# Weights as one array of units by partition, x, p and norm vectors with features on partitions: a two-layer decoder trunk on one core

## What is computed

```python
for i in range(2):
    f = swiglu(rms_norm(h, ffn1_pre_g[i]), ffn1_w_gu[i], ffn1_w_down[i])   # 1024 -> 2*2816 -> 1024
    h = h + 0.5 * rms_norm(f, ffn1_post_g[i])
    u = rms_norm(h, mix_pre_g[i]); ...   # u @ w_in[i] (5120 columns), two attentions, two branches, w_out
    h = h + rms_norm(merged @ w_out[i], mix_post_g[i])
    f = swiglu(rms_norm(h, ffn2_pre_g[i]), ffn2_w_gu[i], ffn2_w_down[i])
    h = h + 0.5 * rms_norm(f, ffn2_post_g[i])
    gate = sigmoid(rms_norm(h, ple_pre_g[i]) @ w_ple_gate[i])
    h = h + rms_norm((p[i] @ w_ple_proj[i]) * gate, ple_post_g[i])
```

## Time and profile before

| | before |
|---|---|
| median of 3 runs | 1174.01 us (1173.98 to 1174.2) |
| span of the profiled execution | 1172.6 us, so 1.4 us less than that median |
| busy: PE, PE's weight loads, DVE, ACT, POOL | 1164.0, 983.8, 850.0, 721.0, 53.0 us |
| DMA packets | 138655, 215.37 MB, mean 184 GB/s |
| of them under 2 KB | 97904 |

### The profile page before, as it was taken

The page is one execution under the profiler, slowest core; times in us unless marked ns, Lnnn a source line. Parts: engine busy times, 40 slices in busy tenths (PEclk is TensorE's granted clock), DMA queues, the critical chain, the costliest instruction groups (busy, mean ns, idle before and its releaser), DMA issues.

```text
span 1172.6 us, 17196 instructions
## 1 busy us (share of the span) xinstructions
PE 1164.0 (99%) x6031; PEld 983.8 (84%) x6031; DVE 850.0 (72%) x1290; ACT 721.0 (61%) x1166; POOL 53.0 (5%) x124
## 2 busy tenths in 40 slices
PE   9999999999999999999999999999999999999997
PEld 7888888888888888888888888888888888888886
DVE  6766776977857776676787776678776677677666
ACT  7555556577755755555685655565776566565555
POOL 4000000000000000000100000010000010000002
PEclk9999999999999999999999999999999999999999
DMA  9656564654354555655556565746434446546550
GB/s 296 217 181 212 171 215 164 226 172 152 121 201 146 191 204 185 208 174 211 179 171 198 172 211 179 240 165 198 171 111 179 162 162 215 194 170 209 179 196 37
DMA packets 138655, 215.37 MB, mean 184 GB/s; under 512 B 6958, under 2 KB 97904, under 8 KB 138608
## 3 DMA queue, kind: packets, MB, share of 16 engines
q1 hardware_dynamic: 135808, 208.43, 52.6%
q10 hardware_dynamic: 2576, 6.29, 1.6%
q0 software_dynamic: 224, 0.04, 0.0%
HBM read 213.68 MB, written 1.05 MB: 183 GB/s over the span
## 4 chain that ended last, share of the span: by engine, by line
PE 99%; DMA 0%; DVE 0%; ACT 0%; issue 0%; POOL 0%; POOLq 0%; DVEq 0%; ACTq 0%
PE ps L1673 23%; PE ps L1546 19%; PE ps L1548 18%; PE ps L1547 18%; PE ps L1683 12%; PE ps L1916 3%; PE ps L1593 1%; PE ps L1925 1%; PE ps L1802 1%; PE ps L1817 1%; PE ps L1776 0%; PE ps L1788 0%; DMA raw<-in_w_ple_proj 0%; PE ps L1831 0%; PE ps L1838 0%; PE ps L1803 0%
## 5 line engine op out<-in xcount | busy, mean ns | idle before, releaser
L1106 DVE SCALAR_TENSOR_TENSOR w_lo<-raw,g_layer,w_hi 128x512 fp32r<-128x512 f32 (+1 forms) x504 | 356.3, 767 | 139.2 <-ACT w_hi L644 139.2
L644 ACT ACTIVATE w_hi<-raw,g_layer 128x512 fp32r<-128x512 f32 (+1 forms) x524 | 346.7, 732 | 113.6 <-PE ps L1683 97.0
L1673 PE MATMUL ps<-x_both,w_hi 128*128 128x512 f32 x1152 | 287.7, 392 | 0.0
L1673 PEld LDWEIGHTS ps<-x_both,w_hi 128*128 128x128 f32 x1152 | 209.3, 189 | 39.4 <-issue 0.4
L1546 PE MATMUL ps<-w_hi,x_both 128*128 128x512 f32 x576 | 231.6, 402 | 0.0
L1548 PE MATMUL ps<-w_hi,x_both 128*128 128x512 f32 x576 | 225.0, 391 | 0.0
L1547 PE MATMUL ps<-w_lo,x_both 128*128 128x512 f32 x576 | 224.4, 390 | 0.0
L1103 DVE TENSOR_TENSOR w_lo<-raw,w_hi 128x1024 fp32r<-128x1024 f32 x114 | 134.8, 1221 | 61.3 <-ACT w_hi L641 61.3
L641 ACT ACTIVATE w_hi<-raw 128x1024 fp32r<-128x1024 f32 x114 | 114.7, 1053 | 92.7 <-PE ps L1548 92.5
L1683 PEld LDWEIGHTS ps<-x_both,w_lo 128*128 128x128 f32 x1152 | 152.6, 191 | 8.4
L1683 PE MATMUL ps<-x_both,w_lo 128*128 128x256 f32 x1152 | 156.0, 283 | 0.0
(11 more groups left out here) (230 smaller groups left out, 1041.7 us busy)
## 6 DMA issues: line engine op xcount, KB each, us to landing
raw<-in_ffn_w_gu SPq DMA_DIRECT2D x170, 512.0 KB, 4.6
raw<-in_ffn_w_down SPq DMA_DIRECT2D x88, 512.0 KB, 4.0
raw<-in_w_in SPq DMA_DIRECT2D x80, 512.0 KB, 4.5
raw<-in_w_out SPq DMA_DIRECT2D x16, 512.0 KB, 4.1
raw<-in_w_ple_gate SPq DMA_DIRECT2D x16, 512.0 KB, 4.1
raw<-in_w_branch_sb SPq DMA_DIRECT2D x8, 512.0 KB, 4.1
raw<-in_w_branch_diff SPq DMA_DIRECT2D x8, 512.0 KB, 4.2
raw<-in_ffn_w_gu SPq DMA_DIRECT2D x12, 256.0 KB, 7.8
```

The costliest lines, as they stand in the source:

```text
L644: last = act.activation(w_hi[:, s, part], raw[:, s, part], ACT.Copy, scale=g_layer[:, g:g + 1])
L1106: last = dve.scalar_tensor_tensor(out=w_lo[:, s, part], in0=raw[:, s, part], scalar=g_layer[:, g:g + 1], in1=whi[:, part], op0=ALU.mult, o ...
L1673: mm = pe.matmul(dst, w_hi[:, s, cols], x_both[:, :, 4 * half + k, :], start=half == 0 and k == 0, stop=stop and k == 3, skip_group_check= ...
```

## The change

The arrays are laid out before the launch: all weight units in one array `w_units` (unit, 128 partitions, 2048), in the order of use; x, p and the norm vectors also with features on partitions (`x_cols`, `p_cols`, `g_cols`). x in its own layout is still loaded into h. SP's loads become one loop. x and p are no longer turned at the start, nor p for the second layer; the norm vectors arrive as one DMA.

```diff
@@ SP
-            (loads of each weight by its own slices: load_gu, load_deep, load_ffn, w_in)
+            for k in range(2):
+                sp_.dma_start(p_raw[:, k, :], a["p_cols"][0, :, k, :]).then_inc(p_in[k], 16)
...
+                    sp_.dma_start(raw[:, slot(u), piece(u, k)], a["w_units"][u, :, piece(u, k)]
+                                  ).then_inc(piece_in[u][k], 16)
+            def load(u, s):
+                sp_.wait_ge(split_done, u + 1)
+                for half in (slice(0, D), slice(D, UNIT)):
+                    sp_.dma_start(raw[:, s, half], a["w_units"][bass.ds(u, 1), :, half].rearrange("o p n -> p (o n)")
+                                  ).then_inc(raw_in[s], 16)
             load_pieces(U_PROJ, (1, 3))
             for u in range(1, PIECED):
                 load_pieces(u)
+            for u in range(PIECED, 2 * SLOTS):
+                load(u, slot(u))
+            with sp_.Fori(2, DEPTH * UNITS // SLOTS) as c:
+                for s in range(SLOTS):
+                    load(SLOTS * c + s, s)
@@ POOL
-            pool.dma_start(g_rows[0:2 * KD, :], a["ffn1_pre_g"].rearrange("l (k p) -> (l k) p", p=P)
...
+            pool.dma_start(g_all[:, :, :], a["g_cols"][:, :, :]).then_inc(g_in, 16)
@@ ACT
-            load_x(0)
-            load_x(2)
+            def load_x_cols(idx):
+                act.dma_start(x_raw(idx), a["x_cols"][:, idx % 2, idx // 2, :]).then_inc(xt_in[idx], 16)
+            def load_x(t):
+                act.dma_start(h[:, t, :], a["x"][0, t * P:(t + 1) * P, :]).then_inc(h_loaded[t], 16)
+            load_x_cols(0)
+            load_x_cols(2)
...
-                act.activation(p_hi[:, :, toks], p_bank(i, t)[:, :, toks], ACT.Copy).then_inc(p_high, 1)
+                act.activation(p_hi[:, ks, :], p_raw[:, ks, :], ACT.Copy).then_inc(p_high, 1)
...
+                if (i, n) == (0, 0):
+                    act.wait_ge(h_loaded[t], 16)
                 act.wait_ge(h_ready, 16 * i + 4 * n + 2 * t + 2)
...
+            high_p(0, slice(0, 1))
             high_piece(U_PROJ, 0)
-            high_p(0, 0, slice(0, P))
             high_piece(U_PROJ, 2)
-            high_p(0, 1, slice(P, SEQ))
+            high_p(0, slice(1, 2))
             high_piece(U_PROJ, 1)
+            load_x_cols(1)
             high_piece(U_PROJ, 3)
+            load_x_cols(3)
+            high_inputs(0, 0, 0, (0,))
+            act.wait_ge(layer_g, 1)
+            high_piece(1, 0)
+            load_x(0)
+            high_piece(1, 1)
             load_x(1)
-            high_inputs(0, 0, 0, (0,))
-            act.wait_ge(first_g, 1)
-            high_piece(1, 0)
-            high_piece(1, 1)
-            load_x(3)
             high_piece(1, 2)
@@ DVE
             def start_layer(i):
+                dve.memset(neg_init[:, :], -LAM_INIT[i])
+                dve.tensor_scalar(g_layer[:, 32:33], g_all[:, i, 32:33], 1.0 - LAM_INIT[i], None, ALU.mult)
+                dve.tensor_copy(g_layer[:, 0:32], g_all[:, i, 0:32]).then_inc(layer_g, 1)
...
             low_piece(U_PROJ, 3)
-            keep_first_gain()
+            dve.wait_ge(g_in, 16)
+            start_layer(0)
             low_inputs(0, 0, 0, (0,))
+            dve.wait_ge(layer_g, 1)
             low_piece(1, 0)
             low_piece(1, 1)
-            keep_gains()
@@ PE
-WARM_UP = (13, 3)
+WARM_UP = 16
...
-                            before = turned_at(0, 0, *{(0, 1): ((1,), (1,)), (1, 0): ((3,), (1,))}.get((s, t), ((), ())))
...
-                before_last()
...
-                beside = {(0, 1): lambda: (turn(0, 0, 0), turn_first_gain()), (0, 3): lambda: turn(0, 0, 2),
-                          (1, 3): turn_gains}
...
-            turn_p(0, (0,))
-            warm_up(WARM_UP[1])
-            turn_p(0, (1,))
```

More of the change, by code:

```diff
@@ L20 @@
 DEPTH, SEQ, D = 2, 256, 1024
-PLE, FF = 256, 2816
+PLE, FF, D_IN = 256, 2816, 5120
 SB_HEADS, SB_D = 8, 64
@@ L216, in trunk_kernel @@
         x_split = sem("x_split")
-        h_loaded = [sem(f"h_loaded{n}") for n in range(2 * TT)]
+        h_loaded = [sem(f"h_loaded{t}") for t in range(TT)]
+        xt_in = [sem(f"xt_in{n}") for n in range(2 * TT)]
         h_ready = sem("h_ready")
@@ L408, in _ @@
         def _(sp_):
[L409 to L431, removed]
+            for k in range(2):
+                sp_.dma_start(p_raw[:, k, :], a["p_cols"][0, :, k, :]).then_inc(p_in[k], 16)
             def load_pieces(u, ks=range(4)):
                 for k in ks:
-                    dst = raw[:, slot(u), piece(u, k)]
@@ L617, in _ @@
             for k in (0, 2):
[L618 to L622, removed]
-            load_x(0)
-            load_x(2)
+                act.dma_start(raw[:, slot(U_PROJ), piece(U_PROJ, k)], a["w_units"][U_PROJ, :, piece(U_PROJ, k)]
+                              ).then_inc(piece_in[U_PROJ][k], 16)
+            def load_x_cols(idx):
[4 more added lines that the diff above has]
+            load_x_cols(2)
             act.preload_act_table_set("silu_and_others")
@@ L656, in high_piece, with high_p @@
                                ).then_inc(hi_ready if k % 2 else piece_high, 1)
-            def high_p(i, t=0, toks=slice(0, SEQ)):
-                act.wait_ge(p_turned, nth_p(i, t))
-                act.activation(p_hi[:, :, toks], p_bank(i, t)[:, :, toks], ACT.Copy).then_inc(p_high, 1)
+            def high_p(i, ks):
+                if i:
+                    act.wait_ge(p_in[0], 16 * i + 16)
+                else:
+                    act.wait_ge(p_in[ks.start], 16)
+                act.activation(p_hi[:, ks, :], p_raw[:, ks, :], ACT.Copy).then_inc(p_high, 1)
             def keep_e(i, t):
@@ L1645, in turn_last_ht, with pieced @@
                 mm.then_inc(ht_turned, 1)
-            def pieced(u, k, then=None):
+            def pieced(u, k):
                 def wait():
@@ L1653, in wait, with ffn @@
                         begin(0, u)
-                    if then:
-                        then()
                 return wait
-            def ffn(i, f, q, u0, before_last):
+            def ffn(i, f, q, u0):
                 def flat_gate_up(u, half, step, c=0, first=False):
@@ L1745, in ffn @@
                         for t in range(TT):
-                            before = turned_at(0, 0, *{(0, 1): ((1,), (1,)), (1, 0): ((3,), (1,))}.get((s, t), ((), ())))
-                            if t == 0:
-                                before = {k: pieced(u0 + s, k, before.get(k)) for k in range(4)}
+                            before = {k: pieced(u0 + s, k) for k in range(4)} if t == 0 else None
                             mm = first_gate_up(s, t, before)
@@ L2093, in _, with laid_out, given, deep @@
                     mm.then_inc(gate_done, 1)
-_NAMES = ["x", "p", "positions",
-          "ffn1_pre_g", "ffn1_w_gu", "ffn1_w_down", "ffn1_post_g",
-          "mix_pre_g", "w_in", "diff_lambda", "diff_subln_g", "w_branch_sb", "w_branch_diff", "w_out", "mix_post_g",
-          "ffn2_pre_g", "ffn2_w_gu", "ffn2_w_down", "ffn2_post_g",
-          "ple_pre_g", "w_ple_gate", "w_ple_proj", "ple_post_g"]
+_AS_GIVEN = ["x", "positions", "diff_lambda", "ffn1_post_g", "mix_post_g", "ffn2_post_g", "ple_post_g"]
+def laid_out(inputs):
+    def given(name):
+        return np.asarray(inputs[name])
+    def deep(w):
+        return w.reshape(-1, 2, P, D).transpose(0, 2, 1, 3).reshape(-1, P, UNIT)
+    def ffn(w_gu, w_down):
+        gu = w_gu.reshape(2, 4, P, 2, NC, FC).transpose(4, 0, 2, 1, 3, 5).reshape(NC, 2, P, UNIT)
+        down = deep(w_down)
+        out = [gu[0]]
+        for c in range(1, NC):
+            out += [gu[c], down[c - 1:c]]
+        return out + [down[NC - 1:]]
+    def w_in(w):
+        blocks = w.reshape(2, 4, P, D_IN // W, W).transpose(3, 0, 2, 1, 4).reshape(D_IN // W, 2, P, UNIT)
+        return [blocks[b] for b in W_IN_BLOCK]
+    units = []
+    for i in range(DEPTH):
+        units += [deep(given("w_ple_proj")[i]), *ffn(given("ffn1_w_gu")[i], given("ffn1_w_down")[i]),
+                  *w_in(given("w_in")[i]), deep(given("w_branch_sb")[i]), deep(given("w_branch_diff")[i]),
+                  deep(given("w_out")[i]), *ffn(given("ffn2_w_gu")[i], given("ffn2_w_down")[i]),
+                  deep(given("w_ple_gate")[i])]
+    gains = [given(n).reshape(DEPTH, KD, P).transpose(2, 0, 1)
+             for n in ("ffn1_pre_g", "mix_pre_g", "ffn2_pre_g", "ple_pre_g")]
+    return {
+        "w_units": np.concatenate(units),
+        "x_cols": given("x").reshape(TT, P, 2, 4, P).transpose(4, 2, 0, 3, 1).reshape(P, 2, TT, W),
+        "p_cols": given("p").reshape(DEPTH, SEQ, 2, P).transpose(0, 3, 2, 1),
+        "g_cols": np.concatenate([*gains, given("diff_subln_g").T[:, :, None]], axis=2),
+    }
 def kernel(**inputs):
@@ L2108 @@
     arrays, args = {}, {}
-    for name in _NAMES:
-        x = np.ascontiguousarray(inputs[name])
+    for name, x in {**{n: inputs[n] for n in _AS_GIVEN}, **laid_out(inputs)}.items():
+        x = np.ascontiguousarray(x)
         arrays[f"in_{name}"] = x
```

165 lines of the change are left out of this document (39 added, 126 removed).

## The result

The changed kernel took 1176.82 us (median of 8 runs, 1176.41 to 1177.4), the kernel before 1173.91 us on the same chip (8 runs, 1173.61 to 1174.35): a ratio of 1.0024, 95% interval 1.0015 to 1.0034. It is 2.9 us slower, where 1.1 us less was forecast. The spans of the two profiled executions differ by 2.8 us. In what follows "after" is the changed kernel; times between kernels are differences from the kernel before as measured beside each.

What follows compares the result with a forecast made beforehand. PE was taken to bound the kernel, with the start tied to ACT and DVE. Moves of -0.7 us at the start and -0.44 at the second layer, together -1.1, gave 1172.9 us from 1174.01, range 1171.6 to 1175.5.

Steps and rivals of the forecast that it cites:

- What bounds the kernel: Whole kernel: PE, 99% of the chain, bounds it; loads are well ahead in the loops; start and second layer decide.
- The turn of p, 0.44: Second layer, on PE: removing this turn saves 0.44 us, counted in full.
- The tie at unit 3's second half: Start: PE begins this half at 28.44, waiting for DVE's SwiGLU product ending at 28.39; an earlier PE would wait.
- 2.29 us of removed PE work: Start, on PE: four turns of x (1.76) and the norm vectors (0.35 and 0.18) go, together 2.29 us.
- so I keep 8.99: Start of ACT's list: the last piece of unit 0 is read at 8.99 us, as before the change.
- The loads and ACT's list, -0.7: Start, 9 to 26 us: half of h ahead makes a piece 0.6 late, so ACT's list moves by -0.7 us.
- 1.08 us of idle time: ACT's idle stretch before x quarter 1 at 17.86; without it the list can be earlier by 1.08 us, no more.
- h goes first: Rival, loads at the start: all of h goes ahead of the pieces, ACT moves +0.8, time 1174.4; chance 0.16.
- The clock: Rival, start of PE: the clock rises later; 1175.5 if the other 21 matmuls of the first product run low; chance 0.07.
- a sign of being wrong: List of wrong signs: among them, matmuls 0.43 us apart after 8 us.
- the loop: Rival, SP's single loop of loads: it makes every unit late, time over 1176.4; chance 0.02.
- the longer half of the clock's case: Rival, start of PE: 12 more matmuls at the low clock, 1177.9; with the loop, chance 0.05 of over 0.2% slower.

Runs made afterwards that it cites:

- e4: The kernel after, with two unused tensors putting every other on-chip tensor back at its old address; 1.2 us faster than after.
- e3: The kernel after, with units 0 to 3, the x quarters and the first p read from unbroken sources; 2.0 us faster than after.
- e15: The kernel after, with only the two h loads issued later; 0.75 us faster than after.
- e8: The kernel before, with 32 unused bytes ahead of os_hi; 0.9 us slower than before.
- e5: The kernel after, with separate arrays in rows of 4 KB for units 0 to 3 and x, 1 KB for p; 0.8 us faster than after.
- e17: e9 with POOL's transfers of the positions and norm vectors issued behind its constants; median 0.1 us above e9's.
- e9: The kernel after, with e3's unbroken sources, e4's old on-chip places and later h loads; median 1.0 us below before, 3.9 below after.
- e10: e9 with the second quarter of x issued on ACT's queue behind the second p; median 1173.33 us.
- e1: The kernel before, with the one array of weight units and the one load loop alone; over 2 us slower than before.

## Why the prediction was wrong

- **What bounds the kernel: right as to the waits, but not whole.** The start and one place at the second layer were to decide; the mixers, in which PE waits for nothing, cost 1.0 us as well (below). Behind 31 us ACT waits for no DMA, so the loop of loads is no cost: in e4, which has it, equal matmuls start 1.71 us later than before at 40 us and 1.77 later at 400.
- **The turn of p, 0.44: right** (0.45 at 553 us).
- **The tie at unit 3's second half: right.** PE waits 0.23 us there for DVE's product, so none of the 2.29 us of removed PE work came by itself.
- **The step that failed:** "Ahead of it lie the same bytes after the change (p, unit 0, two quarters of x), so I keep 8.99". The bytes were the same, their rows were not: 10.96, +1.97. The rate was taken for a property of the wire; the earlier trace rows showed 392 GB/s for before's rows only. e3 shows it: unbroken sources bring 8.96 back and 2.0 us of time. No row of before showed rows 8 KB apart, so the landing needed a bound on the late side; I gave it none.
- **The loads and ACT's list, -0.7: mis-sized**, +0.19 in its place. The 1.08 us of idle time were won as reckoned, and paid out: 0.90 for a piece of unit 2 and 0.45 for the norm vectors (I took 0, at most 0.2). The rival "h goes first" had the direction right, since moving h away wins 0.75 (e15); the +0.19 lies between the forecast's -0.7 and this rival's +0.8.
- **Counted at nothing and worth 1.0:** removing and adding small tensors shifts all that is allotted behind them. No step looked at it. e4 and e8 show it, 1.2 and 0.9 us.
- **The clock:** it did rise later (matmuls 0.43 apart until 9.78), which I had listed as a sign of being wrong; but eight matmuls ran low, where the rival's price of 1175.5 asked for all 24 of the first product, and PE waited for the late piece, so the clock was not what cost the time. The two rivals with prices around the result, the loop and the longer half of the clock's case, are both refuted: the loss is as large as theirs for other reasons.

The sum by the trace: 2.15 at the start, -0.45 for p, 0.55 and 0.5 in the mixers, 2.75 of 2.8 us.

The Trainium skill, DMA: Bandwidth & Descriptors, section "Latency and other measured facts", says that large powers of two as the distance between rows in the chip's main memory slow DMA copies, that 4 KB more at each row cured it and 192 bytes didn't; it advises a pad of a few KB or unbroken tiles. The page's row begins at a distance of 512 KB. The runs here agree on the unbroken layout, show a loss at 8 KB already, and have 512 bytes more as a part of the cure. The row bears on this change, and I did not weigh it.

What stays open: why before, with rows of 4 KB for unit 0 and x, read the piece at 8.99 when e5, with the same distances there, read it at 10.21 (units 1 to 3 and the norm vectors still differ); by what mechanism the rows slow the transfers, only in the first 10 us; and whether 33 KB of norm vectors delay half a megabyte beside them in more than the one trace of e17.

## What to carry to other kernels

When a change relays arrays, cost the first transfers by how their rows lie and not by their bytes, and give what is read first unbroken sources: that was worth 2 us here, with the same bytes and the same instructions. When a change adds or removes on-chip tensors, look at where the operands of TensorE's weight loads begin, and pad them back if they moved. A saving on the engine that bounds the kernel pays only if its inputs can come sooner; with the sources, places and h mended (e9, e17) the change is 3.8 us faster than as made, though not yet told apart from the kernel before.

## What was not expected of the hardware

- Products with os_hi as their 128x128 operand took 389 ns (median of 32) with os_hi at a multiple of 128 bytes, 392 at 64 beyond one, 395 and 397 at 32 and 96 beyond one. The weight loads themselves stayed at 188 ns.
- DMA engines that were busy 92% moved 191 GB/s with 2 KB taken out of each 8 KB, and 397 GB/s at a share of 1.06 with the same 2 KB packets from unbroken sources. From 10 us on the rows of 8 KB ran at 376 to 389.
- With one transfer of 33 KB in rows of 264 bytes issued beside it, a 256 KB piece was read at 7.93, and at 6.23 in the one trace (e17) where that transfer was issued 1.5 us later; the medians don't confirm it.
- All but one of the runs of the kernel before lie between 1173.5 and 1174.8; the variants scatter by up to 3.65 us over ten (e10, 1172.7 to 1176.35; e1 by 2.9). PE in before has no wait on unit 0 and has some in after, so the scatter of the landings may show there in the time; no run separates this.
